# One rotation over eight PSUM banks in place of two for small results and six for large ones

## What is computed

```
for l in range(2):
    [A | B | C inputs] = RMSNorm(x) @ W_in[l]
    A: band attention (4 heads of 64), with a cache for the samples
    B: retention (4 heads, 64 by 128 states), group norm, swish gate
    C: causal depthwise convolution (width 31), LayerNorm, swish
    x = x + concat(A, B, C) @ W_out[l]
    mk, mv = memory @ Wk[l], memory @ Wv[l]          # prompt only
    x = x + CrossAttention(RMSNorm(x), memory K/V)   # samples use cached K/V, 256 x 1024 each
    x = x + FFN_l(RMSNorm(x))    # layer 0: dense SwiGLU; layer 1: top 2 of 8 experts
y = RMSNorm(x)
```

## Time and profile before

| | |
|---|---|
| Time, median of 3 runs | 1993.51 us (1990.95, 1993.51, 1996.22) |
| Profiled execution: span from the first to the last instruction | 1990.5 us |
| Profiled execution: time around the span | not listed; the fastest run is 0.5 us above the span |
| TensorE matmuls busy | 1775.2 us, 89% of the span |
| VectorE busy | 791.9 us, 40% |
| ScalarE busy | 609.7 us, 31% |
| GpSimd busy | 124.2 us, 6% |
| DMA | 340.28 MB, mean 171 GB/s |

### The profile page before, as it was taken

How to read it: one execution, slowest core, us unless ns; L and a number is a source line. 1 busy time by engine, 2 the same in 40 slices (tenths; PEclk the granted TensorE clock), 3 DMA queues, 4 the chain that set the end, 5 groups by cost and what they waited for, 6 DMA issues and landing times.

```text
span 1990.5 us, 20071 instructions
## 1 busy us (share of the span) xinstructions
PE 1775.2 (89%) x7598; PEld 1222.8 (61%) x7598; DVE 791.9 (40%) x1140; ACT 609.7 (31%) x802; POOL 124.2 (6%) x243
## 2 busy tenths in 40 slices
PE   6998789878798998899977997789999999999997
PEld 3454545645678788644545475478667776667764
DVE  1611323233432333326034133246544565445653
ACT  1113112322422322210230232224443554435542
POOL 2230110000000000213002000000000000000000
PEclk9999889999899998999988999978999999999998
DMA  7534234053532333342531423536878887788873
GB/s 236 162 117 146 91 98 148 32 200 139 178 108 75 127 107 114 105 120 85 185 113 40 147 106 111 228 138 222 269 265 288 280 289 257 265 299 269 296 252 132
DMA packets 174553, 340.28 MB, mean 171 GB/s; under 512 B 6890, under 2 KB 48124, under 8 KB 174224
## 3 DMA queue, kind: packets, MB, share of 16 engines
q1 hardware_dynamic: 162224, 316.17, 46.8%
q0 software_dynamic: 3920, 12.58, 2.2%
q10 hardware_dynamic: 8352, 10.75, 1.6%
HBM read 329.43 MB, written 11.90 MB: 171 GB/s over the span
## 4 chain that ended last, share of the span: by engine, by line
PE 83%; DVE 7%; ACT 6%; issue 2%; DMA 1%; POOL 1%; ACTq 0%; SPq 0%; DVEq 0%; POOLq 0%
PE bank L924 19%; PE bank L963 12%; PE bank L964 12%; PE bank L965 12%; PE bank L1045 10%; PE bank L911 5%; PE bank L1064 3%; PE bank L941 2%; PE bank L1394 2%; DVE arena_parts L715 2%; ACT arena_parts L711 1%; PE bank L1092 1%; ACT arena L1460 1%; PE bank L1365 1%; DMA ring<-in_w_in 1%
## 5 line engine op out<-in xcount | busy, mean ns | idle before, releaser
L963 PE MATMUL bank<-arena_parts,features_parts 128*128 128x512 f32 (+1 forms) x960 | 375.8, 391 | 32.5 <-DVE arena_parts L715 21.6
L964 PE MATMUL bank<-arena_parts,features_parts 128*128 128x512 f32 (+1 forms) x960 | 369.8, 385 | 0.0
L715 DVE TENSOR_TENSOR arena_parts<-ring,arena_parts 128x2048 fp32r<-128x2048 f32 (+1 forms) x116 | 247.2, 2143 | 125.2 <-ACT arena_parts L711 125.2
L924 PE MATMUL bank<-ring,features_T 128*128 128x512 f32 (+1 forms) x672 | 273.7, 569 | 1.2 <-ACT features_T L1460 1.2
L711 ACT ACTIVATE arena_parts<-ring 128x2048 fp32r<-128x2048 f32 (+1 forms) x116 | 206.8, 1795 | 114.9 <-PE bank L965 114.1
L965 PE MATMUL bank<-arena_parts 128*128 128x512 f32 (+1 forms) x612 | 240.2, 392 | 0.0
L963 PEld LDWEIGHTS bank<-arena_parts,features_parts 128*128 128x128 f32 x960 | 184.6, 192 | 70.3 <-issue 16.6
L924 PEld LDWEIGHTS bank<-ring,features_T 128*128 128x128 f32 x672 | 128.8, 193 | 142.5 <-issue 138.1
L964 PEld LDWEIGHTS bank<-arena_parts,features_parts 128*128 128x128 f32 x960 | 184.7, 192 | 30.4
L1460 ACT ACTIVATE arena<-bank 128x512 f32<-128x512 f32 (+3 forms) x160 | 88.0, 562 | 373.7 <-PE bank L924 202.9
L965 PE MATMUL bank<-arena_parts,features_parts 128*128 128x512 f32 (+1 forms) x480 | 181.3, 378 | 0.0
(11 more groups left out here) (272 smaller groups left out, 1878.4 us busy)
## 6 DMA issues: line engine op xcount, KB each, us to landing
ring<-in_moe_w_up SPq DMA_DIRECT2D x40, 1024.0 KB, 5.1
ring<-in_moe_w_down SPq DMA_DIRECT2D x30, 1024.0 KB, 5.5
ring<-in_w_in SPq DMA_DIRECT2D x20, 1024.0 KB, 5.7
ring<-in_moe_w_gate SPq DMA_DIRECT2D x20, 1024.0 KB, 5.2
mem_kv<-in_moe_w_gate SPq DMA_DIRECT2D x20, 1024.0 KB, 5.4
ring<-in_cache_mem_k SPq DMA_DIRECT2D x16, 1024.0 KB, 6.4
ring<-in_cache_mem_v SPq DMA_DIRECT2D x16, 1024.0 KB, 5.9
ring<-in_moe_w_gate SPq DMA_DIRECT2D x20, 768.0 KB, 4.7
```

Source lines behind the costliest of these rows:

```text
L715: nc.vector.tensor_tensor(self.part(s, 1), self.raw(s), self.part(s, 0).bitcast(F32), ALU.subtract).then_inc(self.split, 1)
L924: ins = nc.tensor.matmul(out[:, 0:w], left(k, t), wt[:, k - k0, :], start=(g == 0 and k == k0), stop=(g == len(groups) - 1 and k == k0 + n ...
L963: nc.tensor.matmul(out, left[0], right[0], start=start, stop=False)
L964: nc.tensor.matmul(out, left[0], right[1], start=False, stop=False)
```

## The change

Two counters, one for small and one for large results, are replaced by one list of the eight banks, `idle`. Each job takes the bank at the front of the list and puts it to the back. Since every job does so, this is a rotation over eight banks in the order of the jobs, and `begin` waits for the job eight places before. The list starts anew with banks 6, 7, 0 to 5 in each layer. The feed-forward loops keep their banks. The priming transpose takes the bank of the next norm's first transpose, after waiting for it, in place of bank 7.

```diff
     jobs = []
-    small = [0]
-    big = [0]
+    idle = []
 
     def one(key, who):
-        jobs.append((key, (T[small[0] % 2],), who))
-        small[0] += 1
+
+        idle.append(idle.pop(0))
+        jobs.append((key, (idle[-1],), who))
 
     def product(name, chunks, tiles, who):
         for c in range(chunks):
             for t in range(tiles):
-                jobs.append((name + (c, t), (3 * (big[0] % 2) + t,), who))
-            big[0] += 1
+                one(name + (c, t), who)
...
     for l in range(DEPTH):
+
+        idle[:] = [*T, 0, 1, 2, 3, 4, 5]
         norm(3 * l, range(NT - 1))
...
-                (routed if l % 2 else half_ffn).prime(turn(bank[7][:, 0:P], ident))
+                (routed if l % 2 else half_ffn).prime(turn(begin("hT", 3 * l + 2, 0, 0)[:, 0:P], ident))
```

More of the change, by code:

```diff
@@ L145, in product @@
             for t in range(tiles):
-                jobs.append((name + (c, t), (3 * (big[0] % 2) + t,), who))
-            big[0] += 1
+                one(name + (c, t), who)
     def memory_values(l, c):
         for t in range(2):
-            jobs.append((("mv", l, c, t), (3 * (big[0] % 2) + t,), "a"))
-        big[0] += 1
+            one(("mv", l, c, t), "a")
     def norm(n, tiles=range(NT)):
@@ L163, in first_chunk @@
                 norm(n, (2,))
-            jobs.append((name + (0, t), (3 * (big[0] % 2) + t,), "a"))
-        big[0] += 1
+            one(name + (0, t), "a")
     for l in range(DEPTH):
+        idle[:] = [*T, 0, 1, 2, 3, 4, 5]
         norm(3 * l, range(NT - 1))
@@ L172, in psum_jobs @@
         for t in range(NT):
-            jobs.append((("in", l, 1, t), (3 * (big[0] % 2) + t,), "a"))
-        big[0] += 1
+            one(("in", l, 1, t), "a")
         for b in range(2):
@@ L181, in psum_jobs @@
             for t in range(NT):
-                jobs.append((("in", l, c, t), (3 * (big[0] % 2) + t,), "a"))
-            big[0] += 1
+                one(("in", l, c, t), "a")
         product(("mk", l), 2, 2, "a")
@@ L224, in psum_jobs @@
         for t in range(NT):
-            jobs.append((("q", l, 1, t), (3 * (big[0] % 2) + t,), "a"))
-        big[0] += 1
+            one(("q", l, 1, t), "a")
         for j in range(4):
@@ L253, in psum_jobs @@
             one(("pos", l), "v")
-        big[0] = 0
     return jobs
```

## The result

The changed kernel takes 1914.62 us (median of four runs, 1910.14 to 1916.11), beside 1993.1 for the kernel before: a ratio of 0.9608, 95% interval 0.9589 to 0.9627. The profiled executions differ by 82.2 us (spans 1990.5 and 1908.3): that of the changed kernel is the fastest of its four runs, the other three lie at 1914.56 and above, so that gains read stage by stage come out some 4 us too large in all.

What follows compares the result with a forecast made beforehand. TensorE, carrying 83% of the time, bounds the kernel; its pauses for banks can go. Terms sum to 31.2 (layer 0) and 27.8 (layer 1), together 59.0: 1990.5 - 59.0 + 3.0 = 1934.5, said as 1934 us, range 1920 to 1955.

Steps and rivals of the forecast that it cites:

- A: Mixer's keys, heads, scores and transposed probabilities: waits for banks go, 4.2 us a layer, bounds 1 and 5.
- B: Retention scores: all filled long before VectorE needs them, so the result product starts 4.0 us sooner a layer.
- C: Retention's result product to second half of memory values: 17.5 us long, gaining 7.5 in layer 0, 5.8 in layer 1.
- D: Clock of the memory values: TensorE reaches them without a pause, gaining 1.4 us in layer 0, 0 in layer 1.
- E: Mixer results transposed: with six banks ready ScalarE copies without waiting for refills, 1.35 us a layer.
- F: Cross attention up to its result: query, score and probability banks no longer in pairs, 1.7 us a layer.
- G: Four passes over the cached memory: eight key banks filled in one run, 10.0 us a layer; 6 if VectorE's copies were late.
- H: Last norm: the third tile's transposes no longer wait 0.78 for a bank, 0.75 us a layer.
- rival 3: TensorE's clock falls after gathered pauses and stays at 1.2 GHz: 140 us lost in all, 2074 us; chance 0.03.
- rival 2: DMA of slabs limits the passes: passes three and four keep their length, 9 us lost, 1943 us; chance 0.06.
- rival 4: Takes effect only in part, a late copy holding some eight-back bank in the retention stage: 1960 us; chance 0.03.
- rival 1: VectorE becomes the bound, the output projection keeping its distance from its steps: 17.4 us lost, 1952 us; chance 0.12.

Runs made afterwards that it cites:

- The delays: Identity transposes added ahead of the cross queries (changed kernel, five: 1919.28 us; kernel before, thirteen: 1992.80) or the dense loop (changed kernel, eight: 1920.21; sixteen: 1926.16).
- delays of 1.7 us a layer: Changed kernel with sixteen identity transposes between the halves of the cross attention's output projection, ahead of the dense loop: 1926.16 us.

## Why the prediction was too small

Stage by stage between the two profiled executions, forecast and measured, layer 0 / layer 1:

| step | forecast | measured |
|---|---|---|
| A | 4.2 / 4.2 | 7.6 / 8.1 |
| B | 4.0 / 4.0 | 4.0 / 4.0 |
| C | 7.5 / 5.8 | 8.6 / 6.8 |
| D | 1.4 / 0 | 1.3 / 0 |
| E | 1.35 / 1.35 | 1.4 / 1.4 |
| F | 1.7 / 1.7 | 1.3 / 1.2 |
| G | 10.0 / 10.0 | 12.6 / 12.6 |
| H, with the router's product in layer 1 | 0.75 / 0.75 | 0.8 / 2.6 |
| start (the wait for a slab of weights 6.8, not 8.1; chance, in the repeated executions the stage starts at 170.9 before and 172.7 after) | 0.3 / 0 | 1.1 / 0 |
| output projection to queries | 0 / 0 | 0.5 / 0.7 |
| dense loop and next projection | 0 | 5.4 |

- **The bank waits were right.** B is exact, E and H in layer 0 within 0.1. In A the keys and heads gave 2.2 (2.1 forecast), the transposed probabilities 1.27 (1.25). Without the cross product G is 10.6. What was mis-sized is A's scores: 1.68, where I had 0.46 and a part of 0.4, since the row for the 16 products hid a wait and an overlap; and in C the stretch from the result product to the memory values, 16.4 us in every kernel that rotates there, not the 17.5 that I had added up: the third tile took 4.9 (233.32 to 238.18), near the 4.6 that 40 products make at half of 0.23, and I had put 6.
- **The step that failed is the clock.** The prediction changed it at one place (D), said of the feed-forward loops "I give them nothing", and otherwise priced each stretch at its old length; rival 3 let the clock move only to the worse. The cross product gave 2.0 a layer, the dense loop 5.4, the first memory values, which stand in A, 1.4 and 1.9, the router's product 2.3 (10.4 to 8.1): some 15 of the 23 us that the profiled executions gained beyond the forecast. The delays show that for the product and the loop the moment of a pause decides and not the banks; for the memory values and the router's product, kernels with the same banks there gave both lengths. So that part of the gain was luck of where this kernel's pauses fall, and the memory values' part luck of the one profiled execution (13.84 there, 15.29 in layer 1 of the next).
- **The range** was too narrow for that: delays of 1.7 us a layer moved the time by 8 beyond their own length (some 3 of it ahead of them in the profiled execution), so terms exact to 0.1 us can't bring it under some 10.
- **The rivals.** No wait for slabs entered the passes (rival 2), their clock is 1.00 (rival 3), every stage gained (rival 4). VectorE bounds the retention up to the result product, but C, D and E came (rival 1).

## What to carry to other kernels

Where one engine waits only for a result to be emptied, a rotation over all banks in the order of the fills takes the waits away without another instruction, and they can be counted from the timeline beforehand; four banks already give most of it where nobody holds a result long. A change that moves pauses also moves TensorE's clock, in either direction: take the price of each low stretch from the rows, put that sum into the range on both sides, and judge a part of a change by several kernels that have it and by several executions of each. If a pause can't be removed, harmless transposes through it can keep the clock up, here for 10 us more; for the loop, which has pauses of its own, they gained nothing.

## What the runs showed that I had not expected

- The same pause of 3.67 us before the same 16 transposes left the clock low for about 3, 7 or 10 us (product 7.0, 9.0 or 9.4), and a delay of 0.53 us turned the first into the last.
- Score products on alternating row halves take 1.68 us for 16, in another order 2.13.
- A row of matmuls can hide a wait: 0.30 us stood only in the rows of the weight loads.
